# Decoder layer with sparse attention and a two-level mixture of experts: VectorE order, order of loads, slots of the weight ring, second products in quarters and a new router

## What is computed

```python
xn = rms_norm(h, norm1_g)
proj = xn @ w_in        # q, kv, gates, pool, conv (3 parts), 3 x 1024 merge gates
y_nsa  = nsa_mixer(q, kv, gates, ...) @ w_nsa_proj     # compressed, selected and window attention, 8 heads
y_pool = pool_mixer(u, pool_w, pool_scale) @ w_pool_proj
y_conv = short_conv_mixer(conv_h, conv_b, conv_c, conv_w) @ w_conv_proj
merged = mg[:, :, 0] * y_nsa + mg[:, :, 1] * y_pool + mg[:, :, 2] * y_conv
h = h + merged @ w_o
h = h + hier_moe(rms_norm(h, norm2_g), ...)
return rms_norm(h, final_norm_g)
```

```python
g_sel = argmax(g_logits); e_in = e_logits[tok, g_sel]
top_v, top_i = top_k(e_in, 2)
top_w = softmax(top_v) * softmax(g_logits)[tok, g_sel]
for e in range(32):     # every expert, D_EXPERT = 256
    out += combine[:, e:e+1] * ((silu(xt @ w1[e]) * (xt @ w3[e])) @ w2[e])
```

## Time and profile before

| what | value |
|---|---|
| median of 3 runs | 449.24 us |
| the profiled execution | 447.81 us |
| its span (first to last instruction) | 446.0 us |
| TensorE busy | 381.3 us (85%) |
| VectorE busy | 200.6 us (45%) |
| ScalarE busy | 149.1 us (33%) |
| GpSimd busy | 10.2 us (2%) |
| data moved | 140.26 MB, mean 314 GB/s |
| L428, split of a chunk on VectorE, mean of 28 | 2220 ns |
| L421, high part on ScalarE, mean of 28 | 1851 ns |
| expert chunk loads on SP's queue | 96 of 1024 KB |

### The profile page before, as it was taken

One profiled execution on the slowest core, in us unless ns is written; L12 is line 12 of the kernel. 1 busy time (PEld: TensorE's weight loads), 2 busy tenths in 40 slices (PEclk: granted clock), 3 DMA queues, 4 the chain that ended last, 5 costly groups with the idle time before them and its releaser, 6 DMA issues.

```text
span 446.0 us, 6430 instructions
## 1 busy us (share of the span) xinstructions
PE 381.3 (85%) x2508; PEld 247.6 (56%) x2508; DVE 200.6 (45%) x381; ACT 149.1 (33%) x240; POOL 10.2 (2%) x31
## 2 busy tenths in 40 slices
PE   2999999399999999999978797979897877758972
PEld 2999998277777777888763342425342422314320
DVE  0946486878698775783562212212022222102113
ACT  5724421555575634342311212122130302103014
POOL 2000000200000000000110000000000000000001
PEclk9999999799999999999999999999999999969998
DMA  8988998224422585558997994899999999999972
GB/s 305 411 332 334 421 416 371 94 96 141 143 94 96 184 315 175 220 193 331 417 414 301 420 419 165 324 425 416 422 420 421 418 421 422 420 417 422 423 306 94
DMA packets 21190, 140.26 MB, mean 314 GB/s; under 512 B 2608, under 2 KB 2992, under 8 KB 5040
## 3 DMA queue, kind: packets, MB, share of 16 engines
q1 hardware_dynamic: 20160, 138.34, 77.7%
q10 hardware_dynamic: 1008, 1.62, 1.0%
HBM read 138.90 MB, written 1.05 MB: 314 GB/s over the span
## 4 chain that ended last, share of the span: by engine, by line
PE 57%; DMA 16%; SPq 14%; DVE 6%; ACT 3%; issue 3%; POOL 0%; POOLq 0%; ACTq 0%; DVEq 0%
SPq L534 14%; DMA ring<-in_experts 12%; PE bank L1556 6%; PE bank L1331 5%; PE bank L1332 5%; PE bank L1333 5%; PE bank L1529 3%; PE bank L1591 3%; PE bank L1582 3%; PE bank L1190 3%; PE bank L1192 3%; PE bank L1191 3%; DMA ring<-in_front 3%; PE bank L1452 2%; PE bank L1454 2%
## 5 line engine op out<-in xcount | busy, mean ns | idle before, releaser
L428 DVE TENSOR_TENSOR part<-ring,part 128x2048 fp32r<-128x2048 f32 (+1 forms) x28 | 62.2, 2220 | 28.0 <-ACT part L421 27.9
L1556 PE MATMUL bank<-ring,kv 128*32 128x512 f32 x512 | 61.4, 605 | 11.8 <-DVE kv L1128 6.4
L421 ACT CAST part<-ring 128x2048 fp32r<-128x2048 f32 (+1 forms) x28 | 51.8, 1851 | 44.1 <-DMA ring<-in_front 44.1
L1142 DVE TENSOR_TENSOR h<-h,bank 128x512 f32<-128x512 f32 x32 | 22.0, 688 | 71.6 <-PE bank L1591 71.6
L1591 PE MATMUL bank<-gab,vbd 128*128 128x512 f32 x64 | 31.7, 618 | 12.3 <-ACT gab L779 12.3
L1331 PE MATMUL bank<-part,xhi 128*128 128x512 f32 x96 | 39.6, 413 | 0.0
L1582 PE MATMUL bank<-ring,hidT 128*32 128x512 f32 x256 | 32.7, 618 | 7.0 <-ACT hidT L776 5.2
L1556 PEld LDWEIGHTS bank<-ring,kv 128*32 128x32 f32 x512 | 14.0, 110 | 43.4 <-issue 25.9
L1333 PE MATMUL bank<-part,xlo 128*128 128x512 f32 x96 | 37.8, 394 | 0.0
L1332 PE MATMUL bank<-part,xhi 128*128 128x512 f32 x96 | 37.8, 394 | 0.0
L1190 PE MATMUL bank<-xhi,part 128*128 128x256 f32 x128 | 36.7, 287 | 0.1
(11 more groups left out here) (231 smaller groups left out, 536.8 us busy)
## 6 DMA issues: line engine op xcount, KB each, us to landing
ring<-in_experts SPq DMA_DIRECT2D x96, 1024.0 KB, 17.9
ring<-in_front SPq DMA_DIRECT2D x30, 1024.0 KB, 6.1
ring<-in_projs SPq DMA_DIRECT2D x4, 512.0 KB, 4.7
ring<-in_front SPq DMA_DIRECT2D x2, 560.0 KB, 5.8
h<-in_x SPq DMA_DIRECT2D x2, 512.0 KB, 4.0
out_y<-att SPq DMA_DIRECT2D x4, 256.0 KB, 2.4
con<-in_consts SPq DMA_DIRECT2D x1, 782.0 KB, 11.3
oT<-in_vecs ACTq DMA_DIRECT2D x1, 512.0 KB, 6.3
```

The costliest lines, as they stand in the source:

```text
L421: nc.scalar.copy(high(n, half)[:, 0:c].bitcast(F32R), raw(n, half)[:, 0:c]).then_inc(hi_done, 1)
L428: nc.vector.tensor_tensor(low(n, half)[:, 0:c].bitcast(F32R), raw(n, half)[:, 0:c], high(n, half)[:, 0:c], ALU.subtract).then_inc(split_do ...
L1556: ins = mm(bank[0][CAP * e:CAP * (e + 1)], xgT[:, q, CAP * e:CAP * (e + 1)], expert(j, q, e), start=(q == 0), stop=(q == NQ1 - 1))
```

## The change

- VectorE's order in the front: the scores of round 0 come first; pool scaling and the hidden copy follow them, then weighing, the convolution, scores, the projection split and splits of gate chunk 1; the GELU argument goes to the end of round 0, its product to the end of round 1, ScalarE's tanh into round 1.
- Loads: the CH_BC halves ahead of the first early chunk, gate chunks ahead of most early ones.
- `AT`: chunks 22 to 39 of a round go to slots 0 to 17, 40 to 43 to slots 4 to 7, 44 to 47 to 18 to 21.
- Second products and combining in four column quarters of 256 (`NQT`); a chunk holds both hidden halves of a quarter; a quarter is released when it has been copied.
- Gathers of the next block stand in the waits of the block: 0 and 1 before `hN`, 2 before `hT`, 3 to 5 behind the first quarter; 6 and 7 after two chunks.
- Router: the group logits and each group's experts are rows of eight (`RC` = 40 columns, group row padded with -1e30), tokens on partitions at once; all rows are searched together and masked by the group afterwards; ranks come before counts, and the first gather before the passes are read. Token tile 1 is normalised by GpSimd and ScalarE.
- End: squares by half, quarter, quarter; the last sum on VectorE, half of a product on GpSimd.

```diff
 SLOT_XLO, SLOT_MERGED, SLOT_O, SLOT_XHI = 18, 19, 20, 21
-AT = [*range(SLOTS), *range(13), *range(4), *range(13, SLOTS)]
+AT = [*range(SLOTS), *range(18), *range(4, 8), *range(18, SLOTS)]
 CHUNK_SET = {n: (SET_A, SET_B)[i % 2] for i, n in enumerate(SPLITS)}
...
 NQ1 = KT
-NQ2 = 2 * HT
+NQ2 = NQT
...
@@ -476,18 +497,20 @@
             front_chunk(CH_UH, 1)
             projections(0)
             projections(1)
-            early(SLOT_FREE, SLOT_FREE + 1)
             front_chunk(CH_BC, 0)
             front_chunk(CH_BC, 1)
-            early(SLOT_FREE + 1, SLOT_PROJ)
+            early(SLOT_FREE, SLOT_FREE + 1)
             front_chunk(CH_MG, 0)
+            early(SLOT_FREE + 1, SLOT_FREE + 2)
+            front_chunk(CH_MG, 1)
+            early(SLOT_FREE + 2, SLOT_PROJ)
             sp.wait_ge(hidp_full, 2)
-            early(0, 2)
-            front_chunk(CH_MG, 1)
+            early(0, 1)
+            front_chunk(CH_MG + 1, 0)
+            early(1, 2)
+            front_chunk(CH_MG + 1, 1)
             sp.wait_ge(hidp_full, 4)
             early(2, SLOT_FREE)
-            front_chunk(CH_MG + 1, 0)
-            front_chunk(CH_MG + 1, 1)
             front_chunk(CH_MG + 2, 0)
...
-            sp.wait_ge(lgT_full, 1)
+            sp.wait_ge(logit_full, 1)
             early(SLOT_XHI, SLOTS)
...
+            pool.wait_ge(vec_in, 16)
+            for half in range(2):
+                c = slice(half * HALF, (half + 1) * HALF)
+                pool.wait_ge(h_done, 2 * half + 2)
+                nc.gpsimd.tensor_tensor(xn2[:, 1, c], h[:, 1, c], g2b[:, c], ALU.mult).then_inc(gained2, 1)
             half_means(4, 24, NT, rstd_done)
...
+            pool.wait_ge(vec_in, 32)
+            nc.gpsimd.tensor_tensor(fin[:, 1, 0:HALF], h[:, 1, 0:HALF], fing[:, 0:HALF], ALU.mult).then_inc(gained_half, 1)
+            pool.wait_ge(ssq_done, 3 * NT + 2 * NT)
+            nc.gpsimd.tensor_tensor(stat[:, 28:30], stat[:, 28:30], stat[:, 14:16], ALU.add).then_inc(means_done, 1)
+            pool.wait_ge(means_done, 2)
+            nc.gpsimd.tensor_tensor(stat[:, 30:32], stat[:, 28:30], stat[:, 32:34], ALU.pow).then_inc(rstd_last, 1)
...
                     act.wait_ge(merge_done, NT * (n - 1) + t + 1)
+                else:
...
                 take_pT(4 * i + 2)
+                if i == 1:
+                    act.wait_ge(gelu_in, 1)
...
-            act.wait_ge(lgT_full, 1)
-            nc.scalar.copy(lgT, bank[0][:, 0:T]).then_inc(lgT_done, 1)
+            act.wait_ge(gained2, 2)
+            act.wait_ge(rstd_done, 2)
+            nc.scalar.activation(xn2[:, 1], xn2[:, 1], ACT.Copy, scale=stat[:, 27:28]).then_inc(xn2_done, 1)
...
+                for qt in range(NQT):
+                    act.wait_ge(ye_full, b * NQT + (qt + 1))
+                    nc.scalar.copy(yN[:, qt * QC:(qt + 1) * QC], second_out(qt, slice(0, P))).then_inc(yn_done, 1)
...
+            for n, (qt, c0, c1) in enumerate(((1, 0, 2 * QC), (2, 2 * QC, 3 * QC), (3, 3 * QC, D))):
+                for t in range(NT):
+                    act.wait_ge(add_done, passes * (NT * NQT * NB) + (NT * qt + t - NT))
+                    nc.scalar.activation((kv, qflat)[t][:, c0:c1], h[:, t, c0:c1], ACT.Square,
...
             for i in range(N_LOOP):
                 scores(4 * i)
                 scores(4 * i + 1)
+                if i == 0:
+                    mixed_pool()
+                    hidden_read()
                 weigh(4 * i)
                 weigh(4 * i + 1)
-                if i > 0:
+                if i == 0:
+                    convolved()
+                else:
                     take_o(i - 1)
                     for t in range(NT):
                         merge(i - 1, t)
-                have_low(dve, CH_MG + i + 1, 0)
+                    have_low(dve, CH_MG + i + 1, 0)
                 scores(4 * i + 2)
                 scores(4 * i + 3)
+                if i == 0:
+                    projection_low(0)
                 weigh(4 * i + 2)
                 weigh(4 * i + 3)
+                if i == 0:
+                    have_low(dve, CH_MG + i + 1, 0)
                 have_low(dve, CH_MG + i + 1, 1)
                 if i + 1 < N_LOOP:
                     projection_low(i + 1)
+                if i == 0:
+                    gelu_argument()
+                if i == 1:
+                    gelu_product()
...
-            for t in range(NT):
-                dve.wait_ge(h_done, 4)
-                nc.vector.scalar_tensor_tensor(xn2[:, t], h[:, t], stat[:, 26 + t:27 + t], g2b, ALU.mult, ALU.mult).then_inc(xn2_done, 1)
+            dve.wait_ge(h_done, 4)
+            nc.vector.scalar_tensor_tensor(xn2[:, 0], h[:, 0], stat[:, 26:27], g2b, ALU.mult, ALU.mult).then_inc(xn2_done, 1)
...
+                ins = nc.vector.scalar_tensor_tensor(lg[:, t * RC:(t + 1) * RC], bank[(0, 3)[t]][:, 0:RC], stat[:, 26 + t:27 + t], rb[:],
...
+            def first_largest(top, gap, key, big, of, vals, inc):
+                step(nc.vector.tensor_reduce(top, rows(vals), AX.X, ALU.max))
+                ins = nc.vector.tensor_tensor(rows(gap), rows(vals), per_row(top), ALU.subtract)
+                if inc:
+                    ins.then_inc(sub_done, 1)
+                    dve.wait_ge(sub_done, 1)
+                else:
+                    step(ins)
+                step(nc.vector.scalar_tensor_tensor(rows(key), rows(gap), 0.0, rk, ALU.is_equal, ALU.mult))
+                step(nc.vector.tensor_reduce(big, rows(key), AX.X, ALU.max))
+                step(nc.vector.tensor_tensor(rows(of), rows(key), per_row(big), ALU.is_equal))
+            first_largest(top1, gap1, key1, big1, first, lg, True)
+            step(nc.vector.scalar_tensor_tensor(left, first, NEG, lg, ALU.mult, ALU.add))
+            first_largest(top2, gap2, key2, big2, second_of, left, False)
+            nc.vector.tensor_tensor(behind, top2, top1, ALU.subtract).then_inc(sub_done, 1)
+            step(nc.vector.tensor_tensor(both, first, second_of, ALU.add))
...
             dve.wait_ge(rank_full, 1)
             step(nc.vector.scalar_tensor_tensor(rank, bank[1][:, 0:NT * NE].rearrange("p (t e) -> p t e", t=NT), 1.0, mask, ALU.add, ALU.mult))
...
+                dve.wait_ge(count_full, 1)
...
+                nc.vector.tensor_copy(npass[:], pcnt[:, 1:2]).then_inc(passes_done, 1)
+            def select_tokens(b, bb):
...
                 ins.then_inc(sel_step, 1)
...
+            def select_weights(b, bb):
                 dve.wait_ge(sel_step, b + 1)
-                dve.wait_ge(comb_ready, NT)
+                dve.wait_ge(comb_ready, 1)
...
+                        dve.wait_ge(comb_done, b * (NT * NQT) + (NT * qt + t + 1))
+                        hv = h[:, t, qt * QC:(qt + 1) * QC]
+                        nc.vector.tensor_tensor(hv, hv, combined(t), ALU.add).then_inc(add_done, 1)
...
+            select_tokens(0, 0)
+            count_passes()
+            select_weights(0, 0)
...
+            nc.vector.tensor_tensor(fin[:, 1, HALF:D], h[:, 1, HALF:D], fing[:, HALF:D], ALU.mult).then_inc(gained, 1)
+            dve.wait_ge(ssq_done, 3 * NT + 3 * NT)
+            dve.wait_ge(means_done, 1)
+            nc.vector.tensor_tensor(stat[:, 28:30], stat[:, 28:30], stat[:, 16:18], ALU.add).then_inc(means_done, 1)
+            dve.wait_ge(rstd_last, 1)
...
-                ins = mm(bank[0][HD * (k % 2):HD * (k % 2) + HD, 0:T], rw[:, k], h2T[:, k], start=(k < 2), stop=(k >= KT - 2))
-            ins.then_inc(lgT_full, 1)
+                for t in range(NT):
+                    ins = mm(bank[(0, 3)[t]][:, 0:RC], h2T[:, k, t * P:(t + 1) * P], rw[:, k], start=(k == 0), stop=(k == KT - 1))
+            ins.then_inc(logit_full, 1)
...
-            pe.wait_ge(lgT_done, 1)
-            for t in range(NT):
-                c = t * (GROUPS + NE)
-                ins = mm(bank[3][:, c:c + GROUPS + NE], lgT[:, t * P:(t + 1) * P], fold2, start=True, stop=True)
-            ins.then_inc(logit_full, 1)
-            keep_busy(9)
+            keep_busy(6)
             pe.wait_ge(mask_done, 1)
-            for t in range(NT):
-                ins = mm(bank[2][:, 0:NE], ones, mask[:, t], start=(t == 0), stop=(t == NT - 1))
-            ins.then_inc(count_full, 1)
             mm(bank[1][:, 0:NE], tri, mask[:, 0], start=True, stop=True)
             mm(bank[1][:, NE:2 * NE], tri, mask[:, 1], start=True, stop=False)
             mm(bank[1][:, NE:2 * NE], ones, mask[:, 0], start=False, stop=True).then_inc(rank_full, 1)
+            for t in range(NT):
+                ins = mm(bank[6][:, 0:NE], ones, mask[:, t], start=(t == 0), stop=(t == NT - 1))
+            ins.then_inc(count_full, 1)
...
+            pe.wait_ge(xn2_done, NT)
+            pe.wait_ge(sel_step, 1)
+            gather(0, 1, 2, 3, 4, 5)
             pe.wait_ge(passes_done, 1)
             passes = pe.value_load(npass[0:1, 0:1], min_val=1, max_val=MAXPASS)
...
                     for q in range(NQ1):
-                        if q == 4:
-                            gather(6)
```

(26 more changed lines are left out.)

263 lines of the change are left out of this document (113 added, 150 removed).

## The result

The kernel after takes 429.44 us (median of 4 executions: 429.04, 429.43, 429.46 and 2138.73) against 449.99 us for the kernel before: ratio 0.953, 95% interval 0.948 to 0.958. Ratios and intervals leave out two disturbed executions, that of 2138.73 and one of 668.96 of the kernel before, measured beside a_best. Forecast were 430.7 (426.0 to 436.5). The profiled executions took 429.46 and 447.81, 18.35 us apart; the working had 18.5. The first reading is the pair of strips of the page, as in the earlier trace rows; a slice is 10.7 us now.

A forecast was written before the change was run, and what follows sets the result against it. TensorE work bounds up to about 200 us, then loads of 96 expert chunks. Gains 7.9 + 0.7 + 8.0 + 1.85 = 18.5 us from 447.81 give 429.3, or 430.7 on the median's scale; range 426 to 436.5.

The forecast's parts named there:

- rival (d): Expert stage: TensorE's clock falls to 1.2 GHz when loads become the limit and stays there; 463 us; chance 0.04.
- Part 1, front: Before round 0: scores first on VectorE removes TensorE's 6.96 us hole before the first transpose; gain 7.9 us (6.6 to 9.1).
- Part 2, router: Router: first gather starts 1.15 us earlier, 0.7 of it reaching the first weight product; gain 0.7 us.
- Part 3, slot reuse: Expert loads: new slot list leaves 0.2 of 8.2 us of DMA holes; gain 8.0 us, 4.0 with blocks of 23.4.
- Part 4, block: Expert block: quarters and gathers moved into waits shorten it from 23.4 to 20.7 us (19.2 to 23.4).
- Part 5, tail: Behind the last chunk: a quarter product, one combining and 256-column steps take 1.85 us off 6.7 (0 to 2.5).
- (a): Front: the hole only moves from unit 0 to units 2 and 4; gain 4 instead of 7.9, 434.6 us; chance 0.08.
- (b): Expert stage: block stays at 23.4 us, quarters costing more waits; DMA hole moves behind chunk 40; 434.7 us; chance 0.08.
- (c): Front, expert stage and tail: both (a) and (b), and nothing from the tail; 440.5 us; chance 0.04.
- (e): Front: the change doesn't do what it says, the gate load is still last; 438.6 us; chance 0.03.

The follow-up runs named there:

- a_best: Kernel after with GpSimd's last product made early, last-block gathers replacing fillers in the chunk waits, and the third combine ahead of the last quarter product: 429.40 us.
- b_front: Kernel before with only the new front: VectorE order, load order and moved ScalarE steps; 441.64 us, ratio 0.981.
- a_oldfront: Kernel after with the old order of VectorE, loads and ScalarE in front: 440.64 us.
- a_oldloads: Kernel after with the old order of loads alone, the first gate chunk's halves two and three chunks later in the queue: 429.61 us.
- a_latesplit: Kernel after with both of GpSimd's mix splits behind the convolution, so none lies beside the weighing of unit 0: 429.91 us.
- a_countfirst: Kernel after with the count of passes ahead of the ranks, and the passes read by TensorE ahead of the first gather: 430.35 us.
- square of four kernels: Old or new slot list with long or short blocks; slots' hole 9.4 us (old, long), 4.3 (new, long), 5.2 (old, short), 0.1 (new, short).
- b_slots: Kernel before with only the new slot list, blocks still 23.4 us: 445.61 us, ratio 0.990.
- a_oldfront_fill: Kernel after with the old front and 5 more filler products (results unused) in the router's waits: 441.29 us, ratio 0.979.

## Why the prediction was right

**Strips.** Two readings of the earlier trace rows in the prediction are off: the dip in the second half of the loads is a 4, not a 5, with a 7 ahead of it, and the clock's second half has one slice with a 6, not two. The first isn't used in a sum; the second was an argument for rival (d).

**Part 1, front.** Right in value and in mechanism: weighing unit 0 held to 79, TensorE at unit 2 from 87.98 (forecast 88.2) after a wait of 0.72 (1.1), the next round from 98.85 (99.1), loading from 193.84 (194). b_front and a_oldfront show that it arrives whole. Wrong in a part that cost nothing: the earlier gate chunk, which I used to let the scores start, is hardly needed (0.3 us in a_oldloads), as the score products end only at 73.3; nor does the hold cost anything (a_latesplit), as the gate products end when it does. By the rule that I took from the Trainium skill (GPSIMD Engine Reference, Specifications) the scores, which read PSUM and one SBUF operand, would not be held, and the trace agrees: 0.60 us beside GpSimd's subtraction, as without it.

**Part 2, router.** The gather starts 12.13 us behind the last addition instead of 13.19, 1.06 earlier (1.15 forecast), the first weight product 0.4 (0.7), the hole 0.5 (0.7). The steps on 80 elements took 0.24 (0.25). a_countfirst puts 0.7 of it on the ranks going first. What I had not seen is that a fall of the clock reaches the end from here, as it does from the last block (a_oldfront).

**Part 3, slot reuse.** 9.3 us instead of 8.0. The step that missed is the measure: I took the hole from the DMA share (8.2), and a queue can be busy and move little: in 272 to 280 the share was 0.44 and the rate 152 GB/s, 0.36 of 421. By bytes the hole was 9.4. The mechanism and the point from which it decides are shown by the square of four kernels, and the bound of 4 us left with a long block by b_slots (4.3).

**Part 4, block.** 20.4 us (226.90, 247.29, 267.68) against 20.7. The split of it was not as I thought: I counted on the gathers lying in TensorE's idle time; they gave 1.0; 2.0 are left for the quarters and the rest of the block's changes.

**Part 5, tail.** The term that failed: 0.57 us instead of 1.85. A quarter product and two combines are behind the last chunk (2.34, I had one, 1.05), since the third combine stands behind the fourth quarter product in the program. After that the length is not set by the columns but by other engines: six squares in a row on ScalarE, and GpSimd's product between the last of them and the sum, in the timeline of the kernel after:

```profile
417.27 2.34 PE L1656 MATMUL bank<-gab,vbd 128*128 128x256 f32 x8
...
419.40 1.30 POOL L631 TENSOR_TENSOR att<-h,con 128x512 f32<-128x512 f32 x1
...
420.11 1.14 DVE L1225 TENSOR_TENSOR att<-h,con 128x512 f32<-128x512 f32 x1
420.11 0.41 ACT L824 ACTIVATE qT<-h 128x256 f32<-128x256 f32 x1
...
420.65 0.65 POOL L633 TENSOR_TENSOR stat<-stat 128x2 f32<-128x2 f32 x1
```

**Sum.** 7.8 + 0.5 + 9.3 + 0.2 (rate and rest) + 0.6 = 18.4 against 7.9 + 0.7 + 8.0 + 1.85 = 18.5: two terms missed by 1.3 each, in opposite directions. That the total is within 0.2 us is luck; that it is within the range is not.

**Rivals.** (a) fell: TensorE waits 0.72 us for unit 2 and nothing is lost behind it. (b) and (c) fell with the block of 20.4; b_slots shows what (b) would have cost. (d) fell: the clock sinks in the load-bound blocks and comes back. (e) fell, and a_oldloads shows that it could not have come true: the gate load last costs 0.3 us. What the rivals lacked is a short fall of the clock at a place where loads or the end wait for TensorE: 1 to 3 us in the router, 1.3 in the last block of a_oldfront.

## What to carry to other kernels

When loads bound a stage, a hole behind a reused slot depends on two things at once, the slot's place in the list and the speed of the blocks that empty it: work out both turns, and measure holes in bytes, not in the share of busy queues. A transfer can be used about 2 us after its bytes have stopped, so what stands between those two times on the engine is no lateness. A trace shows one execution: before a difference is put down to an edit, compare the clock of both window by window. For a tail, follow every engine between the last product and the last store; halving the columns of one of them moves little.

## What was not expected of the hardware

**In the router.** In ten of the fourteen profiled kernels the granted clock falls to 1.2 GHz (0.5) in the router, in the other four it doesn't, and the kernels with the same instructions up to there are on both sides. A fall takes 3 to 7 us (in b_front 4 x 0.43/0.5 = 3.4; in a_oldfront 4 x (0.20 + 0.50 + 0.15)/0.5 = 6.8). If it meets the gather, or holds back the ranks as in a_oldfront_fill, the router's hole is 3.9 to 6.2 us (seven of the kernels profiled) instead of 2.8 to 3.5 (the other seven).

**Behind the hole in front.** With the old front TensorE stands still for 7 us, and the clock is low when it starts again, for a time that differs between executions. Windows of the kernel before, and below them of a_oldfront_fill:

```profile
80.00:88.00 8.00, 1.97 (x11) 1.45 (x11) 6.38 (x19) 5.06 (x12) 1.36 (x2) 0.71 0.37 131
88.00:96.00 8.00, 8.00 (x39) 5.83 (x35) 6.23 (x16) 5.43 (x13) 0.00 (x0) 0.86 0.01 3
...
80.00:88.00 8.00, 1.24 (x7) 0.91 (x9) 7.04 (x19) 4.34 (x11) 2.09 (x3) 0.66 0.38 131
88.00:96.00 8.00, 8.00 (x32) 6.01 (x31) 4.73 (x8) 4.91 (x11) 0.00 (x0) 0.70 0.01 3
```

Continuous loading starts at 201.60, 202.06, 202.67 and 203.54 in the four kernels with the old front, and between 193.62 and 194.55 in the ten with the new one; in the kernel after the clock is 1.00 in both windows. So the new front also removes a fall that costs the old one time, and not the same time in each execution.

**The spread.** Three of the four executions of the kernel after lie within 0.42 us, while 35 of the kernel before, measured beside the experiments, spread from 447.28 to 452.39: those with a mean clock of 0.98 took 447.3 to 448.2, those at 0.956 to 0.967 took 450.5 to 452.4. That fits falls of either kind, but no trace of a longer execution was read, so it is argued and not shown. It would explain why the medians lie 20.5 us apart and the profiled pair 18.35: the profiled execution of the kernel before, 447.81, is one of the short ones.
